# Two heads per pass over TensorE's columns in the SSD scan, and cache pages issued from GpSimd's queue

## What is computed

```python
cb = jnp.einsum('bclgn,bcsgn->bcgls', cc, bc)
y_diag = jnp.einsum('bcgls,bcgrls,bcsgrp->bclgrp', cb, decay, xg)
states = jnp.einsum('bcsgn,bcgrs,bcsgrp->bcgrpn', bc, decay_end, xg)
y_off = jnp.einsum('bclgn,bcgrpn,bcgrl->bclgrp', cc, h_prev, jnp.exp(a_cum))
```

```python
k_past = cache_k[page_table].reshape(n_seq, -1, ATTN_N_HEADS, 2, ATTN_HEAD_DIM)
v_past = cache_v[page_table].reshape(n_seq, -1, ATTN_N_HEADS, ATTN_V_DIM)
```

## Time and profile before

| | us |
|---|---|
| median of 3 runs (1665.15 to 1666.52) | 1665.21 |
| the profiled execution | 1660.28 |
| its span, first to last instruction | 1658.4 |
| mean granted clock of TensorE | 0.953 |
| TensorE busy with products, share of the span | 95% |

### The profile page before, as it was taken

One profiled execution on the slowest core, in us unless ns is written; L12 is line 12 of the kernel. 1 busy time (PEld: TensorE's weight loads), 2 busy tenths in 40 slices (PEclk: granted clock), 3 DMA queues, 4 the chain that ended last, 5 costly groups with the idle time before them and its releaser, 6 DMA issues.

```text
span 1658.4 us, 29697 instructions
## 1 busy us (share of the span) xinstructions
PE 1570.6 (95%) x12252; PEld 1490.1 (90%) x12252; DVE 944.6 (57%) x1577; ACT 717.6 (43%) x1590; POOL 16.5 (1%) x20
## 2 busy tenths in 40 slices
PE   7999789997999999999999999998989999999997
PEld 6999556996899999999998988887878999999997
DVE  5667777799536742245346868852235752344435
ACT  5435445899425541243224436653245542134321
POOL 0000010000000000000000000000000000000000
PEclk8999999998899999999999999997579999999998
DMA  4222100564221322222222134431412322232221
GB/s 147 82 77 90 39 21 14 204 229 178 77 92 62 115 90 80 99 102 90 90 89 78 64 106 150 141 128 65 139 59 69 103 90 90 77 109 96 77 102 52
DMA packets 46088, 160.15 MB, mean 97 GB/s; under 512 B 5122, under 2 KB 7554, under 8 KB 45954
## 3 DMA queue, kind: packets, MB, share of 16 engines
q1 hardware_dynamic: 45954, 158.25, 27.9%
HBM read 142.07 MB, written 16.16 MB: 95 GB/s over the span
## 4 chain that ended last, share of the span: by engine, by line
PE 78%; DVE 11%; ACT 5%; DMA 4%; issue 2%; SPq 0%; DVEq 0%; ACTq 0%
PE GP L514 17%; PE GP L515 17%; PE GP L516 17%; PE WP L514 5%; PE WP L515 5%; PE WP L516 5%; PE WP L897 2%; DMA sssm<-hs 1%; PE GP L848 1%; DMA hs<-ssm_in 1%; DVE wL L1380 1%; PE GP L672 1%; PE WP L870 1%; ACT ht L1121 1%; PE GP L659 1%
## 5 line engine op out<-in xcount | busy, mean ns | idle before, releaser
L514 PE MATMUL GP<-hidH,wH 128*128 128x260 f32 x1408 | 414.5, 294 | 4.6 <-DVE hidL L1561 4.6
L514 PE MATMUL GP<-aH,wH 128*128 128x260 f32 x1376 | 395.9, 288 | 11.3 <-DVE aL L1406 5.8
L515 PE MATMUL GP<-hidL,wH 128*128 128x260 f32 x1408 | 401.9, 285 | 0.0
L516 PE MATMUL GP<-hidH,wL 128*128 128x260 f32 x1408 | 401.1, 285 | 0.0
L515 PE MATMUL GP<-aL,wH 128*128 128x260 f32 x1376 | 392.1, 285 | 0.0
L516 PE MATMUL GP<-aH,wL 128*128 128x260 f32 x1376 | 391.7, 285 | 0.0
L1380 DVE TENSOR_TENSOR wL<-wraw,wH 128x1024 fp32r<-128x1024 f32 x216 | 260.8, 1222 | 100.9 <-ACT wH L1003 100.5
L1003 ACT ACTIVATE wH<-wraw 128x1024 fp32r<-128x1024 f32 x216 | 225.4, 1053 | 153.7 <-DMA wraw<-wblk 152.9
L514 PEld LDWEIGHTS GP<-hidH,wH 128*128 128x128 f32 x1408 | 269.5, 191 | 10.4 <-DVE hidL L1561 5.5
L514 PEld LDWEIGHTS GP<-aH,wH 128*128 128x128 f32 x1376 | 262.6, 191 | 14.4 <-issue 11.1
L515 PEld LDWEIGHTS GP<-hidL,wH 128*128 128x128 f32 x1408 | 269.9, 192 | 1.9 <-issue 1.5
(11 more groups left out here) (268 smaller groups left out, 2228.5 us busy)
## 6 DMA issues: line engine op xcount, KB each, us to landing
wraw<-wblk SPq DMA_DIRECT2D x216, 512.0 KB, 3.4
hs<-ssm_in SPq DMA_DIRECT2D x16, 512.0 KB, 3.6
sssm<-hs SPq DMA_DIRECT2D x16, 512.0 KB, 4.5
ktile<-kcache SPq DMA_DIRECT2D x16, 512.0 KB, 4.0
vtile<-vcache SPq DMA_DIRECT2D x16, 512.0 KB, 5.6
hT<-x_t SPq DMA_DIRECT2D x4, 520.0 KB, 6.5
kt_out<-kT SPq DMA_DIRECT2D x4, 520.0 KB, 6.6
vt_out<-vT SPq DMA_DIRECT2D x4, 520.0 KB, 5.1
```

The costliest lines, as they stand in the source:

```text
L514: pe.matmul(out, lh, rh, start=first, stop=False)
L515: pe.matmul(out, lh, rl, start=False, stop=False)
L516: return pe.matmul(out, ll, rh, start=False, stop=last)
```

## The change

In the scan a pair's two heads now share one loop: both `seg_sum`s of the next pair stand first, then one wait for both heads' decay matrices, then the 8 products, alternating between the heads for each chunk. Their counters `yd_mm` are raised by the last product of each head. The 32 page loads leave SP's loop and stand, in page order, at the end of GpSimd's stream, each behind the wait that frees its buffer: key page n behind the score of page n - 2, value page n behind the `page_values` that read its buffer before. SP keeps the weight loads and the stores.

```diff
@@ block.sync
-        sp.wait_ge(pt_in, 16)
-        def page(n, cache, dst, i, s):
-            idx = sp.value_load(ptile[0:1, n:n + 1], min_val=0, max_val=cache.shape[0] - 1)
-            sp.dma_start(dst[:, i, :, :].rearrange("p h k -> p (h k)"),
-                         cache[bass.ds(idx, 1), :, :].rearrange("o p n -> p (o n)")).then_inc(s[i], 16)
         stream(kb, kvb)
-        sp.wait_ge(done, PLACE["kv", 0, 0])
-        for n in range(2):
-            page(n, kcache, ktile, n, kp_in)
         for t in range(37):
             if t % 2 and t < STEPS:
                 load(kvb + t // 2)
-            if t - 1 in SPREAD_AT:
-                for n in range(2 * SPREAD_AT[t - 1] + 2, 2 * SPREAD_AT[t - 1] + 4):
-                    if n < NB * PAGES:
-                        sp.wait_ge(ss_s, n - 1)
-                        page(n, kcache, ktile, n % 2, kp_in)
-            if t == 23:
-                sp.wait_ge(ss_s, NB * PAGES)
-                for n in range(4):
-                    page(n, vcache, vtile, n, vp_in)
-            if PAGES_AT.get(t - 1, NB) + 2 < NB:
-                b = PAGES_AT[t - 1]
-                sp.wait_ge(pv_mm, b + 1)
-                for n in (2 * b + 4, 2 * b + 5):
-                    page(n, vcache, vtile, n % 4, vp_in)
@@ block.gpsimd
+        def page(n, cache, dst, i, s):
+            idx = pool.value_load(ptile[0:1, n:n + 1], min_val=0, max_val=cache.shape[0] - 1)
+            pool.dma_start(dst[:, i, :, :].rearrange("p h k -> p (h k)"),
+                           cache[bass.ds(idx, 1), :, :].rearrange("o p n -> p (o n)")).then_inc(s[i], 16)
+        pool.wait_ge(pt_in, 16)
+        pool.wait_ge(done, PLACE["kv", 0, 0])
+        for n in range(NB * PAGES):
+            if n >= 2:
+                pool.wait_ge(ss_s, n - 1)
+            page(n, kcache, ktile, n % 2, kp_in)
+        pool.wait_ge(ss_s, NB * PAGES)
+        for n in range(NB * PAGES):
+            if n >= 4:
+                pool.wait_ge(pv_mm, n // 2 - 1)
+            page(n, vcache, vtile, n % 4, vp_in)
@@ block.tensor, the scan
-                for e in range(2):
-                    k = 2 * n + e
-                    if k % 8 < 6:
-                        seg_sum(k + 2)
-                    pe.wait_ge(md_s, k + 1)
-                    if q < 2 and e == 0:
-                        pe.wait_ge(h_s, g * NCH + q + 1)
-                    for c in range(NCH):
+                if q < 3:
+                    seg_sum(2 * n + 2)
+                    seg_sum(2 * n + 3)
+                pe.wait_ge(md_s, 2 * n + 2)
+                if q < 2:
+                    pe.wait_ge(h_s, g * NCH + q + 1)
+                for c in range(NCH):
+                    for e in range(2):
                         ins = pe.matmul(G[n % 2][64 * e:64 * e + 64, c * P:(c + 1) * P],
                                         xdt[:, c, (2 * q + e) * 64:(2 * q + e) * 64 + 64],
-                                        dec[:, k % 4, c * P:(c + 1) * P], start=True, stop=True)
-                    ins.then_inc(yd_mm, 1)
+                                        dec[:, (2 * n + e) % 4, c * P:(c + 1) * P], start=True, stop=True)
+                        if c == NCH - 1:
+                            ins.then_inc(yd_mm, 1)
```

## The result

| | before | after |
|---|---|---|
| median of 4 runs, us | 1665.87 (1665.15 to 1674.71) | 1648.24 (1645.46 to 1649.73) |
| the profiled execution | 1660.28 | 1649.56 |
| its span | 1658.4 | 1647.9 |

After to before is 0.9885, 95% interval 0.9858 to 0.9912 (14.7 to 23.7 us). The medians differ by 17.6 us, where 15.7 was forecast.

The account below looks back on a forecast made before the run. TensorE, busy 95% of the span, was taken as the bound. Scan -5.6, page wait -7.4 and clock -2.7 sum to -15.7, from a median of 1665.2 to 1649.5 us; range 1643 to 1658.

Parts of the forecast that it names:

- (a) to (d): Scan: 16 alternating passes 1.07 us, pairs with seg_sum 3.56, pair 0 gains nothing, pair 3 0.38 late; -5.6 us.
- (e): Attention: TensorE's wait for a value page before the third page_values goes, -7.4 us.
- (f): Attention: without that idle stretch the third page_values and work behind it run at a higher clock, -2.7 us.
- (g): GpSimd's queue: page loads there, with about 0.7 us for wait and page number, land in time; cost 0.
- rival C: Pages from GpSimd's queue land late, from 11.1 us on delaying VectorE's scores and TensorE; 1677 at 15 us; chance 0.08.
- (h): SP's queue: relieved of the pages, it is free for weights and stores; counted as 0.
- Rival B: Scan: the two column halves take turns in strict order, so alternating gains nothing, +1.2 us, 1656.3 in all; chance 0.08.
- D: Scan: TensorE works less, so the clock falls to 0.50 there, costing 14 us: 1663.5, no change; chance 0.07.
- E: Scan: its gain ends at VectorE, 2 us of 5.6 stay, 1653.1; counted within the forecast's 0.70.

Follow-up runs that it names:

- scan alone: Kernel before with only the scan's tensor block of after, page loads still in SP's queue; 0.9953 of before, median 1657.38 us.
- before once more: The unchanged kernel before, profiled a second time; 1661.62 us, scan groups starting 27.39 and 27.26 us apart.
- pages alone: Kernel before with only the 32 page loads moved to GpSimd's queue, scan as before; 0.9935 of before, median 1655.64 us.
- third profile of before: The unchanged kernel before, profiled again to count scan groups at clock 0.50; first states to first product behind the scan 104.4 to 104.6 us.
- the repeat: The changed kernel run again beside the kernel before on the same chip; 0.9880 of before, medians 1644.40 against 1665.78 us.
- head by head: Changed kernel with a pair's 8 products run one head after the other instead of alternating; median 1650.11 us.

## Why the prediction was right, and where it was not

**(a) to (d), the scan.** Right at the full clock, step by step: 16 passes 1.09 (1.07 forecast), pairs 3.53 apart (3.56), no gain at pair 0, 0.38 lost at pair 3 (0.38; VectorE starts head 7 at 233.77, forecast 233.9). A group is 25.57 before and 24.06 after, 1.51 less against 1.47. The scan alone gives 5.3 in span x clock for the 5.6. What the sum left out is the clock: it took the earlier trace rows, at 1.00, for the scan of before, and that was one execution of four. Over the four profiled executions of the old order the scan takes 102.8 in the mean, over the seven that alternate 93.7: 9.1 less, of which 6.0 is 4 x 1.51 and 3.1 is clock. In the runs of the scan alone the clock column fell by about as much, 3.4; that it fell in the scan is shown by the profiled executions only.

**(e) and (f), the page's wait and the clock behind it.** The 7.43 are gone, and the third product takes 3.63 instead of 6.96. Behind it the clock fell all the same, to 0.54 over 3.6 us, as (f) allowed. From the first `page_values` to the end of the last (TensorE busy, clock), in before once more and in after:

```profile
1112.08:1205.80 93.72, 84.25 (x479) 0.68 0.29 96
```

```profile
1108.05:1193.00 84.95, 83.08 (x479) 0.67 0.32 106
```

That is 8.8 in this pair. Over all profiled executions it is 93.8 in the mean of the four with the pages behind the load (92.5 to 95.7), and 83.9 in the mean of the eight others (82.2 to 85.0): 9.9 less, where (e) and (f) had 10.1. The sum came out by luck in part, since the two terms err against each other. TensorE's idle time in this stretch falls by 8.0, more than the 7.4 of (e), because a later token's pages are late too in two of the four; its busy time, which is what the clock gives back, falls by only 1.9, not the 2.7 of (f) (84.25 to 83.08 in the pair above). In the runs of the pages alone the clock column fell by 4.6; where the rest of that lies is not shown. TensorE's wait for value pages, total, count and longest, in the third profile of before:

```profile
PE WP L897 <- DMA vtile<-vcache: 10.8, 2, 7.7
```

**(g) and rival C.** C's condition did not arise: key pages land in 3.6 us, far from the 11.1 at which C would start, and no VectorE row shows a wait for `ktile`. The 0.7 for the wait and the page number was too small: token 0's products end at 1112.86 and GpSimd's load starts at 1114.08, 1.2 us later, which cost nothing here. C's mechanism is real: for 26.1 us of waits on VectorE TensorE stood 14.6 longer (16.2 against 1.6), and with the clock the median grew by 22.4.

**(h) failed, by a little.** "SP, relieved of the pages, is free for weights": it is, but the pages in a second queue overtake the weights and share the DMA engines with them. What is moved past a queue also leaves that queue's order, and that order had kept four pages behind a block. It cost 1.0 and 1.4 us in the two executions of after.

**Rival B** is refuted by the 1.09 and by the 1.01 us a group that alternation alone is worth. The prediction read too much into the rule behind it: the same section of the Trainium skill (TensorE: Matmul & The Clock Gate, Part 3: Packing small matmuls) also lists a measured speed-up of 2.38 for three products side by side in the columns, and the 1.09 here, for what takes 2.04 one after the other, agrees with that. **D** went the other way: the new order has fewer stretches at 0.50 in the scan. The sign named for it, 0.50 inside the scan, did come in group 1 of after (4.58 us for its states, 3.59 in group 2), but the old order shows more of it in three of four executions. **E** did not occur; 24.06 a group is kept to the z stage.

Altogether: scan 6.0 at the full clock and 3.1 of clock, attention 9.9, less 1.2 for the new wait, make 17.8. The medians gave 17.6 at first and 21.4 in the repeat, whose interval (0.9858 to 0.9903) is 16 to 24 us, so they bear the sum out to a few us and no closer. That the forecast's median came out only 1.3 us too high is luck in part: the scan's clock, which it lacked, is partly offset by the new wait, which it lacked too. That the profiled before lay 4.9 below its median was in the text as an offset. Its scan is 6.7 us shorter than that of the three other executions of the old order, so it hid a loss that the change removes; but before once more has that loss and still took only 1661.62, so the offset as a whole is not explained by it.

**Open.** Why the old order of the scan falls to 0.50 in groups 1 to 3 and the new one, head by head or alternating, only in group 1: both wait 1.44 us at a group's start, and the new order is idle longer at pair 0. The kernel head by head shows that alternation isn't needed for it; no run separates the regrouped `seg_sum`s from the one wait for both decays.

## What to carry to other kernels

A load that waits for its slot holds up all that stands behind it in its queue: look for the transfer whose buffer was free long before its issue, and move it ahead, which can be done in the same queue. A second queue frees the order but also lets its transfers overtake; name what they will share the DMA engines with. And where the profiled execution is faster than its median, look for the loss that it lacks before taking it as the base of a sum.

## What was not expected of the hardware

The granted clock explains most of the difference between executions of one program (over 21 runs of before the span spreads by 5.0 us and span x clock by 2.6, as standard deviations): of groups 1 to 3 of the scan, the three profiled executions of before have 0, 3 and 3 with a stretch at 0.50, with the same instructions. GpSimd's loads stand 1.14 us apart (1080.48, 1081.62) and land no later than SP's in the median, key pages in 3.6 us against 4.0, value pages in 4.3 against 5.6; the longest value page took 7.6 against 6.1. A 512 KB load's landing goes from 3.7 to 6.8 us by what another queue has issued in the 5 us ahead of it.
